# A two-layer step with a RWKV-7 scan and experts: key rates, keys' factor, ones, the scan's opening and the order of overflow blocks are moved

## The reference, cut to what matters

```python
for d in range(2):
    logw = -softplus(-(w0[d] + tanh(xw @ w1[d]) @ w2[d])) - 0.5
    decay = heads(exp(-exp(logw)))
    a = heads(sigmoid(a0[d] + (xa @ a1[d]) @ a2[d]))
    k_d = k * (1 + (a - 1) * k_a_h)
    y_d, s_d = wkv_scan(r, decay, k_d, v, -kk, kk * a, s0[:, d], reverse=(d == 1))
    y_sum = y_sum + y_d
    bonus = bonus + sum(r * k_d * r_k, -1, keepdims=True) * v
mean = mean(y_sum, -1)                      # per head
var = mean(square(y_sum - mean), -1)
yn = (y_sum - mean) * rsqrt(var + GN_EPS) * lnx_g + lnx_b
return ((yn + bonus) * g) @ w_o
...
hid = silu(einsum('nd,edf->nef', xt, w1)) * einsum('nd,edf->nef', xt, w3)
y = einsum('nef,efd->nd', hid * gate[..., None], w2)
```

## Time and profile before

| what | us |
|---|---|
| median of 3 runs | 1475.67 (1475.34 to 1478.3) |
| profiled execution, its own time | 1485.73 |
| its span, first to last instruction | 1483.9 |
| PE busy | 1271.5 (86%) |
| DVE busy | 528.9 (36%) |
| ACT busy | 339.2 (23%) |
| POOL busy | 383.9 (26%) |
| mean granted clock of PE | 0.928 |

### The profile page before, as it was taken

The page is one execution under the profiler, slowest core; times in us unless marked ns, Lnnn a source line. Parts: engine busy times, 40 slices in busy tenths (PEclk is TensorE's granted clock), DMA queues, the critical chain, the costliest instruction groups (busy, mean ns, idle before and its releaser), DMA issues. The chain is left out here.

```text
span 1483.9 us, 22069 instructions
## 1 busy us (share of the span) xinstructions
PE 1271.5 (86%) x8819; PEld 883.9 (60%) x8819; DVE 528.9 (36%) x1169; ACT 339.2 (23%) x825; POOL 383.9 (26%) x710
## 2 busy tenths in 40 slices
PE   4899988999999997897687889799977876888887
PEld 2456856778887786354454545555865544545456
DVE  2530095556666664643310111500236233110115
ACT  2351163222222121222211111200145222111111
POOL 0100086445544441100132331000037200424210
PEclk9999988999999999798799999799979986999997
DMA  9852035667656514253499767593300444867652
GB/s 361 217 170 85 1 123 154 181 180 213 215 160 187 160 42 140 95 198 129 169 392 407 282 228 250 199 175 110 103 15 1 162 184 163 324 222 248 230 175 82
DMA packets 200709, 264.70 MB, mean 178 GB/s; under 512 B 93883, under 2 KB 155467, under 8 KB 184992
## 3 DMA queue, kind: packets, MB, share of 16 engines
q1 hardware_dynamic: 163200, 221.63, 44.5%
q0 software_dynamic: 17152, 31.20, 5.8%
q10 hardware_dynamic: 20256, 10.48, 3.4%
HBM read 300.11 MB, written 28.96 MB: 222 GB/s over the span
## 5 line engine op out<-in xcount | busy, mean ns | idle before, releaser
L2064 PE MATMUL psum<-ring,slab 128*64 128x256 f32 x896 | 191.4, 396 | 17.0 <-DMA slab<-moe_w,slab 12.3
L2064 PE MATMUL psum<-slab 128*64 128x256 f32 x832 | 172.2, 382 | 0.0
L2064 PEld LDWEIGHTS psum<-ring,slab 128*64 128x64 f32 x896 | 116.4, 143 | 75.7 <-issue 35.0
L2092 PE MATMUL psum<-ring,ws 128*64 128x512 f32 x224 | 105.7, 652 | 16.9 <-issue 15.0
L2064 PEld LDWEIGHTS psum<-slab 128*64 128x64 f32 x832 | 107.5, 138 | 3.6 <-issue 1.0
L2237 DVE TENSOR_TENSOR ws<-ws,psum 128x256 f32<-128x256 f32 (+1 forms) x28 | 16.9, 604 | 240.6 <-PE psum L2064 117.4
L2092 PE MATMUL psum<-slab,ws 128*64 128x512 f32 x208 | 99.1, 659 | 1.3 <-issue 1.3
L2308 PE MATMUL psum<-slab,ring 128*128 128x384 f32 x256 | 84.5, 494 | 7.2 <-PEq L176 7.2
L2156 POOL DMA_INDIRECT y_rows<-slab x26 | 26.4, 1014 | 248.3 <-DVE slab L2247 229.4
L2501 POOL TENSOR_SCALAR ws<-ws 128x384 f32<-128x384 f32 x32 | 39.4, 1243 | 190.4 <-DVE ws L2571 190.4
L1269 DVE TENSOR_TENSOR ws<-psum,causal 128x512 f32<-128x512 f32 x96 | 63.7, 686 | 47.5 <-PE psum L879 46.4
(11 more groups left out here) (368 smaller groups left out, 2441.3 us busy)
## 6 DMA issues: line engine op xcount, KB each, us to landing
ring<-moe_w SPq DMA_DIRECT2D x84, 1024.0 KB
ring<-ada_w SPq DMA_DIRECT2D x46, 1024.0 KB, 9.1
ws<-inverses SPq DMA_DIRECT2D x48, 256.0 KB, 3.8
slab<-moe_w SPq DMA_DIRECT2D x12, 1024.0 KB, 8.8
ring<-na_w_qkv SPq DMA_DIRECT2D x12, 1024.0 KB
slab<-y_rows SPq DMA_DIRECT2D x12, 512.0 KB, 6.6
ring<-rwkv_w_r SPq DMA_DIRECT2D x4, 1024.0 KB
ring<-rwkv_w_k SPq DMA_DIRECT2D x4, 1024.0 KB
```

Of the source, the lines that this page charges most:

```text
L2064: last = nc.tensor.matmul(k.psum[BT * g:BT * g + BT, h_bank(s, kind), 0:DE], cols_[s % 2][:, c, BT * g:BT * g + BT], w[g][:, c, :], start= ...
L2092: last = nc.tensor.matmul(k.psum[BT * g:BT * g + BT, 5 + half, :], turned_hid[s % 2][:, P * f + BT * g:P * f + BT * g + BT], w[g][:, f, 51 ...
```

## The change

It does the following.

- Overflow blocks are ordered 0, 10, 1, 9, 2, 8, ... over steps 2 to 12 (`SPACED`) instead of 0, 1, 2, ...
- In an experts' step GpSimd first gathers the rows of the step after next and issues two of the three overflow loads of the next step, then puts the last results, then issues the third. `last_rows` and VectorE's copy of it move from the start to step 2.
- Scan: `modulate(0)` moves from before the casts of block 2 to behind the turned states; `bands(1)` from ahead of round 0 to between the two kinds of pairs of round 0; `rows_copy(0)` behind the exponentials of round 1.
- VectorE makes the rates of round 1 itself, after the memsets and the starting states, which now come before the scaling for round 1.
- In the last round GpSimd adds the rates of both directions, and SP loads the ones, once round 10's results are done, and waits for their landing before it issues the output projection's pieces.
- Behind the scan the keys' factor is made by ScalarE (one block ahead), all squares are made before the bonus is copied out, and nothing waits for the ones.

The diff, cut to its core:

```diff
-PAIR = [(0, 1), (2, 3)] + [(4 + j, NE + j) for j in range(OVER)] + [(NE - 1,)]
+SPACED = [j // 2 if j % 2 == 0 else OVER - 1 - j // 2 for j in range(OVER)]
+PAIR = [(0, 1), (2, 3)] + [(4 + j, NE + SPACED[j]) for j in range(OVER)] + [(NE - 1,)]
...
+    rate_late, rate_sums = pair("rate_late"), k.sem("scan_rate_sums")
+    block_in = k.sem("scan_block_in")
...
-            modulate(0)
...
-            for d in range(2):
-                pe.wait_ge(band_ok[d], 1)
-            for part in range(2):
-                bands(1, part)
+            modulate(0)
...
+                if r == 0:
+                    for d in range(2):
+                        pe.wait_ge(band_ok[d], 1)
+                    for part in range(2):
+                        bands(1, part)
...
-            rows_copy(0)
...
+            rows_copy(0)
...
-                dve.wait_ge(rate_ok[d], r + 1)
+                if r == 1:
+                    dve.wait_ge(rate_late[d], 1)
+                else:
+                    dve.wait_ge(rate_ok[d], max(r, 1))
...
-            dve.wait_ge(nkk_ok, DC)
+            dve.wait_ge(state_turned, 1)
             for d in range(2):
-                scaled_ar(d, 1)
-                scaled_kb(d, 1)
-            dve.wait_ge(state_turned, 1)
+                dve.wait_ge(centred[d], 3)
+            for d, b in enumerate(D2):
+
+                nc.vector.memset(b.ak[b.late, :, :, :, b.early], 0.0).then_inc(y_ok[d], 1)
+                nc.vector.memset(b.ab[b.late, :, :, :, b.early], 0.0).then_inc(y_ok[d], 1)
...
             dve.wait_ge(edges_ok, 4)
             for d, (e, n) in enumerate(((k.ep0, 1), (k.epe, 2))):
                 nc.vector.tensor_tensor(k.s0t[:, d, :, :], k.psum[:, 4 * d + 3, :].rearrange("p (c i) -> p c i", c=DC),
                                         e[:, d, :, n:n + 1].to_broadcast([P, DC, HD]), ALU.mult).then_inc(state_ok, 1)
+            dve.wait_ge(nkk_ok, DC)
             for d, b in enumerate(D2):
-
-                nc.vector.memset(b.ak[b.late, :, :, :, b.early], 0.0).then_inc(y_ok[d], 1)
-                nc.vector.memset(b.ab[b.late, :, :, :, b.early], 0.0).then_inc(y_ok[d], 1)
+                q, n, _ = place(1, d)
+                toks = bass.ds(P * n, P)
+                dve.wait_ge(z_read[d], len(Z))
+                dve.wait_ge(band_out[d], 32)
+                nc.vector.tensor_tensor(b.rate, k.act3(S_NKK)[:, bass.ds(2 * q, 2), toks], b.a[:, bass.ds(2 * q, 2), toks],
+                                        ALU.mult).then_inc(rate_late[d], 1)
+                scaled_ar(d, 1)
+                scaled_kb(d, 1)
...
-                pool.wait_ge(first_ok[d], 2)
-                pool.wait_ge(band_out[d], 32)
-                rates(d, 1)
...
+            sums_of_rates = k.act3(S_PB)
+            pool.wait_ge(exp_rest[1], len(ROUNDS))
+            for g in range(4):
+                part = slice(2 * g, 2 * g + 2)
+                nc.gpsimd.tensor_tensor(sums_of_rates[:, part, :], D2[0].a[:, part, :], D2[1].a[:, part, :], ALU.add).then_inc(rate_sums, 1)
...
+            for d in range(2):
+                sp.wait_ge(y_done[d], len(ROUNDS) - 1)
+            sp.dma_start(k.ws[:, 0:P], k.a["c_block"]).then_inc(block_in, 16)
+            sp.wait_ge(block_in, 16)
...
-            pe.wait_ge(block_in, 16)
...
-            sp.dma_start(ones, k.a["c_block"]).then_inc(block_in, 16)
...
-            for g in range(4):
-                nc.gpsimd.tensor_tensor(tb[:, 2 * g:2 * g + 2, :], af[:, 2 * g:2 * g + 2, :], ab[:, 2 * g:2 * g + 2, :], ALU.add).then_inc(rates_sum, 1)
...
+            def key_factor(c):
+
+                nc.scalar.activation(tb[:, c, :], tb[:, c, :], ACT.Identity, bias=omka2[:, c:c + 1],
+                                     scale=k.vec[:, V_KA + c:V_KA + c + 1]).then_inc(bonus_a, 1)
+
+            act.wait_ge(omka2_ok, 1)
+            key_factor(0)
             for c in range(DC):
+                if c + 1 < DC:
+                    key_factor(c + 1)
                 act.wait_ge(less_mean, c + 1)
                 nc.scalar.activation(sq[:, c, :], y[:, c, :], ACT.Square).then_inc(y_squared, 1)
+            for c in range(DC):
                 act.wait_ge(bonus_done, c + 1)
-                act.wait_ge(rates_sum, 4)
...
-
-                dve.wait_ge(rates_sum, c // 2 + 1)
-                nc.vector.tensor_scalar(tb[:, c, :], tb[:, c, :], k.vec[:, V_KA + c:V_KA + c + 1], omka2[:, c:c + 1],
-                                        ALU.mult, ALU.add).then_inc(bonus_a, 1)
...
-                        pe.wait_ge(*((hid_ok, s) if s else (last_ok, 1)))
+                        if s:
+                            pe.wait_ge(*((last_ok, 1) if s == 2 else (hid_ok, s)))
...
-            last_rows()
             turn(0)
             for s in range(PAIRS):
+                if s == 2:
+                    pe.wait_ge(hid_ok, s)
+                    last_rows()
...
-                for kind in range(3):
+            def overflow(s, kinds):
+
+                for kind in kinds:
...
+                more = 2 <= s + 1 < PAIRS - 1
+                if s + 2 < PAIRS:
+                    gather(s + 2)
+                if more:
+                    overflow(s + 1, range(2))
                 if s:
                     put(s - 1)
-                if s + 2 < PAIRS:
-                    gather(s + 2)
-                if 2 <= s + 1 < PAIRS - 1:
-                    overflow(s + 1)
+                if more:
+                    overflow(s + 1, range(2, 3))
...
-            dve.wait_ge(spread_turned, 1)
-            nc.vector.tensor_copy(by_row, k.psum[0:BT, 7, 0:T]).then_inc(last_ok, 1)
...
+                if s == 2:
+                    dve.wait_ge(spread_turned, 1)
+                    nc.vector.tensor_copy(by_row, k.psum[0:BT, 7, 0:T]).then_inc(last_ok, 1)
```

5 lines of the change are left out of this document (2 added, 3 removed).

## The result

The changed kernel takes 1431.46 us (median of four runs, 1427.82 to 1440.53), the one before 1475.51 beside it: ratio 0.9712, 95% interval 0.9662 to 0.9762. The forecast was 1458.8 and a range down to 1454, so the sign was right and the gain was 44.1 us instead of 16.9. In the profiled executions the span went from 1483.9 to 1429.3 us.

A forecast was written before the change was run, and what follows sets the result against it. A chain of stages with barriers bounds the kernel, each edit priced in its own stage. Gains of 4.5 + 5.4 + 6.5 + 0.5 = 16.9 us took the median from 1475.67 to 1458.8, range 1454 to 1467 (8 in 10).

The forecast's parts named there:

- Opening: Scan's opening: rates on VectorE, earlier memsets and modulate(0) in the gap bring the first level to 239.8; gain 4.5 us.
- It is kept: Scan's rounds: the opening's 4.5 us lasts, because the rounds are paced by their own chain.
- Rival B: Scan's opening: gain lost to second pairs waiting for ScalarE and the inverses; remaining gain 0, total 1463.3; chance 0.13.
- since the gap that lowered it is filled: Scan's opening: pairs of direction 0 run at the full clock, at 230.1 instead of 235.42.
- Last round: Scan's last round: GpSimd's four adds, 7.21 us, move into its idle time from 565; cost nothing.
- Behind the scan: Scan's end to output projection: VectorE's block takes 1.6 us instead of 2.10; gain 5.4 us, bounds 3 and 6.5.
- Rival D: Bonus sums to output projection: 64 matmuls at half clock cost 20.7 us, total 1479.5; chance 0.03.
- Experts: Experts' steps: spread blocks and earlier loads gain 6.5 us in layer 0 (bounds 2, 8), 0.5 in layer 1.
- the 8 us that I had named as a sign of being wrong: Layer 0 of the experts: the prediction is wrong if waits of over 8 us stay there.
- The measure is layer 1: Experts: layer 1, with fewer overflowing blocks, is 7.1 us shorter, so not all 11.2 us of waiting come back.
- VectorE's late product: Experts: an aside that after a stall VectorE's product is no longer late; no size of its own.
- Rival C: Experts stay bound by transfers, the ring late after each overflow step; gain 0.5 instead of 7, total 1465.3; chance 0.15.

The follow-up runs named there:

- before2: The kernel before, unchanged, traced a second time on another chip; layer 1 took 173 us with no hold and 10.3 us of waiting.
- after2: The changed kernel, unchanged, run once more in the second comparison: 1437.79 us, 0.9791 of the kernel before.
- a_oldorder: The changed kernel with GpSimd's old order of issues in the experts (put, gather, three overflow loads in one row): 1462.85 us, 0.9966 of the kernel before.
- b_order: The kernel before with GpSimd's new order of issues alone: 1447.01 us, 0.9875.
- b_noempty: The kernel before without layer 1's empty overflow loads from the fifth step on and without the waits for them: 1454.69 us, 0.9921.
- b_putlast: The kernel before with the put issued behind the gather and the three overflow loads, still after waiting for the last step's output: 0.9984.
- a_onhand: The changed kernel with gather and two overflow loads held until the first half of the inner products is done: 1456.96 us, 0.9944 of the kernel before.
- b_afterhand: The kernel before with gather and overflow loads held until TensorE has turned the hidden values: 1502.78 us, 1.0272.
- b_opening: The kernel before with the scan's new opening alone: 1.0006 (0.9979 to 1.0033).
- b_post: The kernel before with rates added by GpSimd in the last round, keys' factor by ScalarE and ones loaded early: 0.9965, 5.1 us faster.
- a_onhand2: The changed kernel with gather and two overflow loads held until half the inner products, again, on a chip that holds signals: 1464.3 us, 0.9854 of before.

## Why the prediction was right, and where it failed

**Opening: path right, sum wrong.** Forecast against trace: pairs 230.1 (230.72), second pairs 236.8 (236.69), first level 239.8 (239.65). That the last two agree to 0.2 us is partly luck, since the whole scan began 1.4 us later than in before; over all traces the first level gained 4.4 us from the scan's start (58.4 to 54.0), near my 4.5. The step that failed is the sentence "It is kept", which took the rounds as paced by their chain alone. They are also paced by the granted clock, and the stretch at 1.2 GHz that the old opening spends ahead of the first level falls into the rounds. Term: 4.5 us forecast, -0.9 measured (interval -4.8 to 3.1 gained). Rival B had the outcome, for another reason: the new stall for ScalarE and the inverses was in my sum (2.1 us, measured 1.43 for the copy and 0.96 for the inverses). That VectorE and GpSimd get in each other's way cost the sum nothing: GpSimd's copy took the delay (2.00 instead of 0.40 us), and its next work waited 3.68 us for TensorE anyway. My claim that the clock stays full "since the gap that lowered it is filled" is the same mistake: it was 1.00 at the pairs of this trace, but a fall came later. Why it falls where it does stays open.

**Last round: right.** GpSimd's adds start at 564.38 and end 18 us before the scan's end; the work that needs them (ScalarE's keys' factor) starts at 590.64.

**Behind the scan: right.** 5.4 forecast, 6.0 in the trace, 5.1 (1.9 to 8.2) in the comparison of this part and the last round's alone; period of a block 1.6 forecast, 1.59 measured. Rival D did not happen.

**Experts: the step that failed most.** 7.0 us forecast with bounds 2.0 less 0.8 to 8 plus 1; 31 us measured on one chip, 46 us in the first pair of traces. The step that failed is the pricing of this stage by the wait for real blocks' weights in layer 0 alone. That wait is real, but its size depends on the trace: at both products of layer 0 it went from 11.9 to 10.5 us in the first pair, where it moved from the inner to the outer product and stayed over the 8 us that I had named as a sign of being wrong, and from 21.5 to 7.9 us between before2 and after2. What I left out is what the order of issues does where nothing is transferred. Layer 1's steps stood in the trace at 13 to 16 us with hardly any wait for loads, and I took them for the floor ("The measure is layer 1") instead of asking what ended the 1.6 us of idleness at each flip. I had even named VectorE's late product, in a parenthesis, and gave it no term; it was 9.4 and 15.5 us of TensorE's time. The floor of a step was 12.5 us. Rival C was wrong: the transfers let the steps go.

Two mechanisms make those long steps, by the chip. On two of the five chips of the experiments, and in the first trace of before, TensorE's signal reaches VectorE about 2.1 us after the last of five issues in a row that lies on the handover; that costs 1.8 us a step (14.3 against 12.5) and 3.5 where the clock falls behind the gap (0.58 over 1315 to 1319 in the step of 16.0 us). On the other three, nothing is held, and steps run into overflow loads that land late, 10.2 to 10.4 us after their issue in before2. The new order avoids both: the first loads are issued 6.7 us earlier, which leaves them 14.75 us, and no row ends on the handover. That the order of issues is what gains in layer 1 is shown by a_oldorder, b_order and the layer times, and by b_noempty that on such a chip the empty loads are the loss. That the row of issues causes the hold rests on traces alone: the late start follows the last issue in b_putlast, and no trace with the row elsewhere has it at this size; no run took only the row away on a chip that holds signals. Why a chip has it stays open.

Why an empty load lands after 4 or after 10 us stays open too. It is not its place behind the put (theory Q): in before2 the put had landed 8.8 us earlier, and the same order of issues gave 3.6 to 5.8 us in every second step. It is not the time of issue alone (theory T): 6.7 us were enough in a_onhand, whose load issued at 1296.89 landed after 4.7 us. In b_afterhand, from the issue at 1306.06 on, it took 2.2 to 4.2 us. A third reason fits the traces, that the load waits for the ring's pieces on the same DMA engines: beside the four of before2, nine of the ten landings of over 9.7 us in layer 1 of a_oldorder, b_opening and b_post lie within 0.3 us of the landing of a piece issued after the load. No run tested it.

The measured time lies outside the stated range because of the experts' term. The fall of the opening's term to zero was inside it.

## What to carry to other kernels

Look for the steps that are longer than their instructions, also where the wait names no transfer, and compare where each row of GpSimd's DMA issues lies against TensorE's handovers. An indirect load that moves nothing still has to land before its waiter goes on (here 10 us over one layer), so issue it early, and read how long each took to land before you blame its place in the queue. When a wait shrinks at one line, add up the waits of all lines that take the same data: it may have moved. Where TensorE's clock fell after a pause, the shortened path moved the fall here and did not remove it: count a gain only when the rounds behind it have kept their length in several traces.

## What the runs showed of the hardware that I had not expected

- One program has several levels by chip: before took 1467 to 1470 us on three chips, 1487 on two and 1475.5 in the first comparison (where the profiled execution, with the hold, took 1485.73 and the others 1471.8 to 1478.3), while the changed kernel and its neighbours took 1431 to 1438 on all. The worth of the change is 2.1% on a chip of the first sort, 2.9% in the first comparison and about 3.5% on the second sort (0.965 for the kernel with the put last; the change itself was not run there), so a ratio from a single chip is not the kernel's.
- On those two chips and in the first trace, five indirect issues in a row on GpSimd, 1.3 us apart, the last at the moment when TensorE's signal is due, went with VectorE's start at 2.0 to 2.1 us behind the turning instead of 0.16, and ScalarE's copy at 2.07 instead of 1.13 (1312.94 less 1310.87 in the first trace, 1288.57 less 1287.44 in before2); with the row's third issue there the delay was 0.14 us (0.30 in a_onhand2). On the other three chips the same rows held nothing.
- An indirect load without data, behind a put and a gather in the same order of issues, landed 10.2 to 10.4 us after its issue in four steps of before2 and 3.6 to 5.8 us after it in the four between; in b_afterhand, with the put landed, 2.2 to 4.2 us.
- VectorE's operations with two inputs from SBUF and GpSimd's work beside them lengthened one another, and either engine was the one that paid: GpSimd's 128x256 copy took 2.00 us instead of 0.40 in after, and VectorE's 128x256 product 1.33 us instead of 0.41 in after2 (at 230.97).
- TensorE was granted 1.2 GHz for about 10 us in the middle of dense work (494 to 506 us, windows of 4 us with 3.85 to 4.00 us busy), after two idle spans of 0.5 to 0.6 us; a_onhand has the same two in its round 8 (0.59 and 0.55 us) and no fall.
